# One of the two sums of each down step moved from ScalarE and GpSimd to VectorE, also beside the key selection

## The reference

```
mix = jnp.concatenate([a_o, s_o], axis=-1) @ w_out
x = x + rmsnorm(mix, g_post)
hdn = jnp.square(jax.nn.relu(rmsnorm(x, g_ffn_pre) @ w_up))
return x + rmsnorm(hdn @ w_down, g_ffn_post)
```

## Time and profile before

| what | value |
|---|---|
| median of 3 runs | 3682.56 us (3680.38 to 3683.88) |
| the profiled execution | 3676.49 us |
| its span in the trace | 3674.8 us |
| mean granted TensorE clock | 0.912 of full speed |
| TensorE busy | 3039.5 us, 83% |
| VectorE busy | 1842.5 us, 50% |
| ScalarE busy | 1637.8 us, 45% |
| GpSimd busy | 1244.2 us, 34% |
| copies of a bank to `part`, adds of it | 390 each |
| sums by VectorE from the bank | 120, and 5 copies |

### The profile page before, as it was taken

The page is one execution under the profiler, slowest core; times in us unless marked ns, Lnnn a source line. Parts: engine busy times, 40 slices in busy tenths (PEclk is TensorE's granted clock), DMA queues, the critical chain, the costliest instruction groups (busy, mean ns, idle before and its releaser), DMA issues.

```text
span 3674.8 us, 47108 instructions
## 1 busy us (share of the span) xinstructions
PE 3039.5 (83%) x15352; PEld 2401.7 (65%) x15352; DVE 1842.5 (50%) x4116; ACT 1637.8 (45%) x2873; POOL 1244.2 (34%) x1149
## 2 busy tenths in 40 slices
PE   7998544647778889996799999968999999699996
PEld 5886421314556668764577886646778888588885
DVE  4432962762357984367685332666772333511112
ACT  3332412522546755575563446745634444322222
POOL 1332620313013561253264114522672112224444
PEclk9999766868879999998899999889999999899998
DMA  4444344546336564354454223343543213544443
GB/s 152 138 140 151 86 128 131 136 133 205 102 130 216 207 248 134 116 200 146 164 182 166 82 79 122 128 171 120 184 165 114 70 61 129 188 146 152 174 154 111
DMA packets 219182, 529.45 MB, mean 144 GB/s; under 512 B 57514, under 2 KB 114924, under 8 KB 192924
## 3 DMA queue, kind: packets, MB, share of 16 engines
q1 hardware_dynamic: 199900, 499.65, 39.6%
q0 software_dynamic: 9824, 18.40, 1.6%
q10 hardware_dynamic: 9216, 8.39, 0.7%
HBM read 399.43 MB, written 134.12 MB: 145 GB/s over the span
## 4 chain that ended last, share of the span: by engine, by line
PE 49%; DVE 12%; issue 10%; ACT 5%; POOL 3%; DMA 3%; SPq 1%; ACTq 1%; POOLq 0%; DVEq 0%
PE r L1620 16%; PE r L1652 12%; PE po L1700 4%; PE tr L1691 3%; ACT junk_a_b L1969 2%; POOL acc_b L2104 1%; PE sc L1668 1%; PE sc L1679 1%; PE sc L1678 1%; PE r L1809 1%; DVE junk_v_b L2343 1%; DVE trial_b L2295 1%; PE tr L1668 1%; PE r L1765 1%; POOL hr_b L2085 1%
## 5 line engine op out<-in xcount | busy, mean ns | idle before, releaser
L2104 POOL TENSOR_TENSOR acc_b<-acc_b,part_b 128x512 f32<-128x512 f32 x375 | 516.1, 1396 | 495.8 <-ACT part_b L1920 494.9
L1652 PE MATMUL r<-ready_b,h_b 128*128 128x512 f32 x2304 | 569.4, 403 | 42.2 <-ACT part_b L1920 38.2
L1652 PEld LDWEIGHTS r<-ready_b,h_b 128*128 128x128 f32 x2304 | 437.4, 193 | 159.2 <-ACT part_b L1920 50.7
L1620 PE MATMUL r<-x_hi_b,ready_b 128*128 128x512 f32 x1536 | 493.6, 395 | 5.4 <-DVE x_lo_b L2209 2.8
L2085 POOL TENSOR_TENSOR hr_b<-hr_b 128x512 f32<-128x512 f32 x128 | 148.4, 1159 | 777.1 <-ACT hr_b L1907 776.8
L1969 ACT ACTIVATE junk_a_b<-score_b,trial_b 128x384 int8<-128x384 f32 (+13 forms) x266 | 347.5, 1306 | 103.5 <-DVE trial_b L2295 102.4
L1620 PEld LDWEIGHTS r<-x_hi_b,ready_b 128*128 128x128 f32 x1536 | 290.8, 189 | 75.8 <-issue 10.1
L1920 ACT ACTIVATE part_b<-r 128x512 f32<-128x512 f32 x390 | 223.5, 594 | 217.1 <-PE r L1652 130.8
L1700 PEld LDWEIGHTS po<-V_sb,pT_b 128*128 128x128 f32 x2176 | 287.5, 192 | 23.1 <-issue 3.1
L1620 PE MATMUL r<-x_lo_b,ready_b 128*128 128x512 f32 x768 | 301.0, 392 | 0.0
L1996 ACT ACTIVATE pT_b<-tr 128x512 f32<-128x512 f32 (+3 forms) x320 | 168.8, 527 | 264.4 <-PE tr L1691 262.6
(11 more groups left out here) (407 smaller groups left out, 6028.6 us busy)
## 6 DMA issues: line engine op xcount, KB each, us to landing
ready_b<-ws_u SPq DMA_DIRECT2D x96, 1024.0 KB, 6.7
ready_b<-ws_d SPq DMA_DIRECT2D x96, 1024.0 KB, 5.0
ws_u<-up_b SPq DMA_DIRECT2D x32, 1024.0 KB, 8.8
ws_d<-dn_b SPq DMA_DIRECT2D x30, 1024.0 KB, 6.5
raw_b<-w_out SPq DMA_DIRECT2D x64, 256.0 KB, 3.2
raw_b<-w_up SPq DMA_DIRECT2D x32, 512.0 KB, 5.5
raw_b<-w_down SPq DMA_DIRECT2D x32, 512.0 KB, 4.1
kv_b<-kv_pages SPq DMA_DIRECT2D x96, 128.0 KB, 3.8
```

Of the source, the lines that this page charges most:

```text
L1620: mm = pe.matmul(x[:], wt[:, c], y[:, k], start=k == n == 0, stop=(k, n) == (KD - 1, 2))
L1652: mm = pe.matmul(x[:], f[:, tok], w[:, col], start=c == n == 0, stop=(c, n) == (KQ - 1, 2))
L2104: pool.tensor_tensor(dst, dst, part[:, add_no[key] % 2, :], ALU.add).then_inc(add_pool, 1)
```

## The change

It touches the one line that says which engine sums h = 0.

```
             for h, i in down_banks(u[1])[2 * u[3]:2 * u[3] + 2]:
                 key = ("D", u[1], u[2], h, i)
-                sum_by[key] = "act" if h or beside_search(u) else "dve"
+                sum_by[key] = "act" if h or (u[1] == 0 and beside_search(u)) else "dve"
                 fill(key, sum_by[key])
                 if u[2] and sum_by[key] == "act":
                     n_add += 1
```

## The result

The changed kernel takes 3717.25 us (median of 4 runs, 3716.02 to 3722.86), the kernel before 3681.47 us on the same chip (4 runs, 3679.53 to 3683.88). The ratio is 1.0100 with a 95% interval of 1.0082 to 1.0117: 1% slower, some 36 us. In the profiled executions the span went from 3674.8 to 3714.7 us, 39.9 more.

The account below looks back on a forecast made before the run. TensorE, busy for 83% of the span, was taken as the bound, with its gaps. Gains of 1.5, 3 and 5.5 us in the three stretches summed to 10 us: 3682.6 - 10 = 3672.6 us, range 3652 to 3692.

Parts of the forecast that it names:

- The bound and the prize: TensorE's work and gaps set the time; its 38.3 us of down-step waits for ScalarE's copies could be saved.
- A: Selection beside down steps of group 1, 174 us with 10.3 of TensorE gaps; forecast gain 1.5 us.
- The prices: Removes 91 ScalarE copies (54 us) and 83 GpSimd adds (107 us); puts 91 sums on VectorE (0.69 us each, 63 us).
- The places: Where VectorE reaches a sum after TensorE wants its bank: 2 to 5 us late in most heavy cycles.
- B: Selection beside the later down steps of group 1, 194 us with 14.7 of TensorE gaps; forecast gain 3 us.
- A late sum costs only once: In each stretch one place decides: TensorE's stream shifts once, and gaps after that point are still saved.
- C: Selection beside down steps of group 2, 240 us with 19.4 of TensorE gaps; forecast gain 5.5 us.
- a wait swallows what comes before it: Only sums since VectorE last waited for a count delay it: two or three per deciding place, 1.4 to 2 us.
- The clock: TensorE's granted clock dips after long waits in the three stretches; gain put at nothing, 5 us at most.
- The slower rival: VectorE becomes the bound beside the selection: 15 us more, 3698 us, or 3690 with half the relief; chance 0.22.
- its point of decision: Slower case decides if the selections of stages 2 and 3 end after 1977 and 2750; they ended at 1969.6 and 2743.4.
- the rival's other sign: Group 2 begins later than its share: the stretch from 1803 to 2510 grows longer.

Follow-up runs that it names:

- e12: Kernel before, with only the eight h = 0 banks of steps 3 and 4 of group 2 summed on VectorE: 3693.15 us, 1.0038 of the kernel before.
- e3: Changed kernel, with VectorE's sums in groups 1 and 2 ahead of the selection unit that follows: 3668.28 us, 0.9963 of the kernel before.
- e2: Changed kernel, with ScalarE's counts in groups 1 and 2 one unit earlier, ahead of the next unit's copies: 3685.39 us, 1.0019 of the kernel before.
- e5: Kernel before, plus an independent VectorE instruction of a sum's length at each of the 91 places: 3692.54 us, 1.0037 of the kernel before.
- e11: Every h = 0 bank on VectorE, group 0 too, with sums in front in groups 0 to 2: 3650.78 us, 0.9922 of the kernel before.
- e1_swap: Changed kernel, with bank h = 1 instead of h = 0 summed on VectorE beside the selection: 3686.0 us, 1.0015 of the kernel before.

## Why the prediction was wrong

**The bound and the prize: right.** TensorE's waits for line 1920 in down steps went from 38.3 us to 0.6, as said, and ScalarE's waits for GpSimd in A to 3.3.

**The prices: right in their bounds.** Line 2223 of the changed kernel, whole span:

```profile
L2223 DVE TENSOR_TENSOR acc_b<-r,acc_b x188: 677/692/693, 1378.8 to 3680.5; 128x512 f32<-128x512 f32 x188
```

A sum takes 692 ns beside GpSimd as elsewhere, and the copies to `part` are 307, the number that was forecast for the adds.

The group of line 2295 in A, changed kernel (busy us, mean ns of one, idle before):

```profile
L2295 DVE SCALAR_TENSOR_TENSOR trial_b<-trial_b,turn_b 128x1 int32<-128x1 int32 x63 | 17.1, 271 | 2.2
```

437 ns became 271 ns, 10.9 us less where 4.5 was the estimate. VectorE was relieved more than forecast, and it did not help.

**The places: right in the main; the size of the new waits: wrong.** The prediction found VectorE 2 to 5 us late in most heavy cycles, and named steps 1 to 4 of group 1 and 0 to 5 of group 2. The waits stand in steps 0 to 3 and 0 to 5, up to 6.5 us each, but also in B, 21.4 us in steps 11 to 15 of group 1, which the list left out. Together they are 72.0 us, where 20 to 30 were forecast. In a single place the lateness was read well; what was not foreseen is how often it is paid.

**The step that failed** is "A late sum costs only once, though: TensorE's whole stream then shifts, and later lateness counts against the shifted stream." It holds if VectorE's times are fixed. They are not. VectorE waits for counts; the count stands behind a copy; the copy waits for TensorE. When TensorE shifts, the copy shifts, the count shifts, and so does the next sum: it is late again by as much. The prediction even had the link in hand and used it for the good direction alone ("where TensorE itself comes earlier, so do the counts that stand behind its U banks"). By its rule the change was to gain 10 us, with 1.5 us in A and 5.5 in C; measured is a loss of 11.3 and 18.6. e12 shows the rule false; e3 and e2, with their controls, show that the loop is the reason in the steps where they take the loss back (steps 1 to 3 of group 1 and 2 to 5 of group 2, 28 us).

**A second step that leans on the first:** "a wait swallows what comes before it". With the loop, VectorE's 133 us of waits for counts were not all slack: they rose to 148 us, in A and C, while in B they fell by 10.

**The clock** was put at nothing with 5 us as its best case. It went the other way: the same 15352 matmuls take 9.3 us more on the page. In steps 3 and 4 of group 2 the granted clock falls to 0.93 and 0.86 from 1.00, and the 98 and 97 matmuls of the windows take 24.35 and 26.05 us, not 22.54: 5.3 us, a third of what the two steps lost (7.0 and 8.4 us).

**The slower rival** had the sign, and its point of decision was passed. The last VectorE instruction of stage 2's selection:

```profile
1982.90 2.12 DVE L2331 SCALAR_TENSOR_TENSOR tie_b<-tie_b,junk_v_b 128x1536 bf16<-128x1536 bf16 x1
```

It ends at 1985.0, past 1977; that of stage 3 ends at 2793.3, past 2750. Group 2 begins later than its share too, the rival's other sign: 20.2 us more lie between the first steps of groups 1 and 2. But the price, 15 us, was less than half, and the reason was another: for the most part not VectorE out of idle time. The load by itself costs 13.4 us with no relief (e5), near the rival's 15; with the sums well placed the same load comes with a gain (e3). The Trainium skill, Perfetto Trace Analysis, Optimizing Scalar/DVE Operations, points from a saturated VectorE to ScalarE. It gave the right sign here, but its condition was not met: VectorE has 50% on the page, 144 of 185 us in A, and e11 is fastest with the most on VectorE. For the moved sums the order within the engine's queue decided more than its share.

**The range** (3652 to 3692) left the time out by 25 us, since no rival had a loss that repeats. All of the rivals' lateness was counted against idle time that would absorb it.

**Left open.** The attention after A (step 7 of group 1) takes 54.6 us, not 50.5. In the kernel before, stage 2's selection ends 7.7 us ahead of the down steps beside it; in the changed kernel it ends with them, and in e3_sum_first (where the step takes 56.0 us) 3 us after them. That goes together, but no run isolates it. Steps 0 and 1 of group 2 lose 9.2 us in a way that neither cut of the loop mends. The loop was cut by moving the sum and by moving the count; shortening one of its legs instead, say ScalarE's 2.0 us count in half, was not tried. Nor is it known why e1_swap fell short.

## What to carry to other kernels

Before you move work onto an engine that runs in a fixed order, list what stands ahead of it in that engine's queue, and follow each of those waits back: if the chain returns to the engine that will wait for the moved work, the loss is the time around the chain less the time of the work, and it is paid in every turn, even though no engine is busy all of the time. Rules such as "a delay costs only once" need the late engine's times to be independent of the delayed one; a rise in *its* waits, though it was given more work, is a sign that they were not. If such a loop appears, move the short instruction ahead of the waiting ones before you give up the change: here that turned +36 us into -10, and with group 0 into -28.

## What the runs showed of the hardware

VectorE's sum from a PSUM bank took 677 to 693 ns in all 188 cases, GpSimd at work or not, while its one-column trial update with two operands in SBUF, 158 ns alone, ran up to 1302 ns and lost 166 ns of its mean in A when half of GpSimd's adds went. The Trainium skill, SBUF — State Buffer, Who interferes with whom, says that a VectorE instruction with two SBUF inputs contends with a GpSimd instruction that reads SBUF, and that one with at most one SBUF input, outside certain modes, does not; both lines agree with that.

The granted clock fell behind waits of TensorE and took the next matmuls with it. After the wait of 4.07 us the window from 2644.36 to 2647.30 has a granted clock of 0.50, the lower of its two levels (1.2 of 2.4 GHz); the six matmuls at 2653.58, after another wait, of 1.98 us, take 2.21 us, six with the full clock 1.65. Over that step the clock is 0.93 and TensorE is busy for 24.35 us with what took 22.54 at 1.00. A gap of TensorE thus cost more here than its own length.
